# A half's second gather waits, in the GpSimd queue, for the half issued ahead of it to land

## The reference

```python
# each sample has 4096 past rows in 32 pages of a pool
phys = page_table[b4, start // PAGE_SIZE]
ks = jnp.where(is_past, pool_sk[phys[..., None], rows, g5], ...)
vs = jnp.where(is_past, pool_sv[phys[..., None], rows, g5], ...)
logits = einsum('btgrd,btgksd->btgrks', q, ks) * SM_SCALE + bias   # masked softmax
o_s    = einsum('btgrks,btgksd->btgrd', p, vs)
```

## Time and profile before

| | |
|---|---|
| median of 3 runs | 897.07 us (895.75 to 898.39) |
| profiled execution, its own time | 897.14 us |
| its span in the trace | 895.1 us |
| TensorE, VectorE, ScalarE, GpSimd busy | 96%, 69%, 42%, 14% |
| granted TensorE clock, mean | 0.994 of 2.4 GHz |
| DMA traffic | 118.31 MB, mean 132 GB/s |

### The profile page before, as it was taken

The page is one execution under the profiler, slowest core; times in us unless marked ns, Lnnn a source line. Parts: engine busy times, 40 slices in busy tenths (PEclk is TensorE's granted clock), DMA queues, the critical chain, the costliest instruction groups (busy, mean ns, idle before and its releaser), DMA issues.

```text
span 895.1 us, 15701 instructions
## 1 busy us (share of the span) xinstructions
PE 861.1 (96%) x6053; PEld 555.3 (62%) x6053; DVE 617.7 (69%) x1148; ACT 372.0 (42%) x885; POOL 121.7 (14%) x130
## 2 busy tenths in 40 slices
PE   9999999999999999999999998998889998999997
PEld 8656665666666666766775776766665766544442
DVE  5698789999988988999657557566766666222222
ACT  6111244211021211014877887776677666211111
POOL 1012110000001011110103131232244320000000
PEclk9999999999999999999999999999999999999999
DMA  9535551422144066630760020000019996521211
GB/s 327 188 118 169 188 206 55 61 50 76 43 135 182 27 208 227 212 126 40 250 227 25 11 86 2 1 1 2 1 53 378 415 416 267 178 84 65 83 70 36
DMA packets 32110, 118.31 MB, mean 132 GB/s; under 512 B 3434, under 2 KB 11772, under 8 KB 22972
## 3 DMA queue, kind: packets, MB, share of 16 engines
q0 software_dynamic: 9360, 68.16, 20.3%
q1 hardware_dynamic: 20316, 46.45, 15.1%
q10 hardware_dynamic: 2360, 2.71, 2.0%
HBM read 108.33 MB, written 13.29 MB: 136 GB/s over the span
## 4 chain that ended last, share of the span: by engine, by line
PE 89%; ACT 4%; DVE 3%; issue 2%; DVEq 1%; ACTq 0%; POOL 0%; POOLq 0%
PE PS L847 36%; PE PS L2210 12%; PE PS L1631 6%; PE PS L1641 6%; PE PS L1661 5%; PE PS L2029 3%; ACT main L1428 3%; PE PS L2090 2%; PE PS L2054 2%; PE PS L813 2%; PE PS L2067 2%; PE PS L829 1%; PE PS L1614 1%; DVE main L1474 1%; DVE main L1483 1%
## 5 line engine op out<-in xcount | busy, mean ns | idle before, releaser
L847 PE MATMUL PS<-main 128*128 128x352 f32 (+1 forms) x1056 | 327.9, 469 | 0.0
L847 PEld LDWEIGHTS PS<-main 128*128 128x128 f32 x1056 | 200.3, 191 | 119.5 <-issue 1.3
L1428 ACT ACTIVATE main<-PS,main 128x512 f32<-128x512 f32 (+3 forms) x192 | 103.8, 561 | 49.2 <-DVE main L1470 24.5
L2210 PE MATMUL PS<-main 128*128 128x512 f32 x256 | 111.6, 593 | 0.0
L434 ACT ACTIVATE main<-PS 128x384 f32<-128x384 f32 x24 | 11.7, 489 | 199.4 <-PE PS L847 195.5
L644 DVE SCALAR_TENSOR_TENSOR main<-main,par 128x1022 f32<-128x1022 f32 (+16 forms) x66 | 83.8, 1270 | 5.3 <-issue 0.4
L1641 PE MATMUL PS<-cst,main 128*128 128x128 f32 x528 | 73.2, 280 | 13.3 <-ACT main L1428 12.8
L2210 PEld LDWEIGHTS PS<-main 128*128 128x128 f32 x256 | 47.9, 190 | 58.1 <-issue 58.0
L603 DVE TENSOR_TENSOR main<-main 128x1024 f32<-128x1024 f32 x64 | 75.5, 1221 | 9.3 <-DMA main<-in_cmp_k_dram,row 6.5
L606 DVE TENSOR_TENSOR main<-main 128x1024 f32<-128x1024 f32 (+2 forms) x96 | 75.0, 781 | 7.2
L1641 PEld LDWEIGHTS PS<-cst,main 128*128 128x128 f32 x528 | 56.7, 140 | 29.7 <-ACT main L1428 23.6
(11 more groups left out here) (328 smaller groups left out, 1039.2 us busy)
## 6 DMA issues: line engine op xcount, KB each, us to landing
main<-in_w_tiles_dram SPq DMA_DIRECT2D x24, 512.0 KB, 3.6
out_dram<-main SPq DMA_DIRECT2D x18, 256.0 KB, 2.0
main<-in_x_prompt_dram SPq DMA_DIRECT2D x8, 512.0 KB, 8.6
main<-in_w_out_dram SPq DMA_DIRECT2D x4, 1024.0 KB, 7.8
main<-in_x_prompt_dram SPq DMA_DIRECT2D x16, 256.0 KB, 2.9
out_dram<-main SPq DMA_DIRECT2D x4, 512.0 KB
diag<-in_win_k_dram SPq DMA_DIRECT2D x8, 256.0 KB
diag<-in_win_v_dram SPq DMA_DIRECT2D x8, 256.0 KB, 7.8
```

The costliest lines, as they stand in the source:

```text
L847: last = pe.matmul(bank(3 * s + j)[:, 0:w], ring[:, s, k * P:(k + 1) * P], xT[:, k, t0:t0 + w], start=(k == 0), stop=(k == KD - 1))
L1428: last = act.activation(prob[:, k % 2, g, h * nk_ * P:(h + 1) * nk_ * P], score_set(k, g)[:, h * nk_ * P:(h + 1) * nk_ * P], ACT.Exp, scal ...
L2210: last = pe.matmul(out_bank(m, h), proj[:, MIX[k], n * P:(n + 1) * P], wo[:, k, h * 512:(h + 1) * 512], start=(x == 0), stop=(x == KD - 1))
```

## The change

From K11 on, every half's second gather (`b2 == 1`) waits until the half that stands ahead of it in the queue has landed, both of its gathers. The first gather of a half has no such wait. K00, K01, V00 and K10 stay as they were. The waits are on GpSimd's own queue, between a half's first and second gather.

```diff
-        def pool_keys(pool, pr, h):
+        def keys_landed(pr, h):
+            return kd_ld[h], 32 * pr + 32
+        def values_landed(p, h):
+            return (vd_ld[2], 32 * p + 32) if h else (vd_ld[p % 2], 32 * (p // 2) + 32)
+        def wait_gather(pool, ahead, b2):
+            if ahead is not None and b2 == 1:
+                pool.wait_ge(*ahead)
+        def pool_keys(pool, pr, h, ahead=None):
             for b2 in range(2):
+                wait_gather(pool, ahead, b2)
                 pool.indirect_dma_start(kd[:, b2, h * 2048:(h + 1) * 2048], None, half_rows("sel_k"),
...
-        def pool_values(pool, pr, h):
+        def pool_values(pool, pr, h, ahead=None):
             for b2 in range(2):
+                wait_gather(pool, ahead, b2)
...
         def pool_decode(pool):
-            def keys(pr, h):
+            def keys(pr, h, ahead):
                 keys_used(pool, pr - 1, 4 * h + 3)
-                pool_keys(pool, pr, h)
+                pool_keys(pool, pr, h, ahead)
...
-            keys(1, 1)
+            keys(1, 1, keys_landed(1, 0))
...
-            values(0, 1)
-            values(1, 0)
+            values(0, 1, keys_landed(1, 1))
+            values(1, 0, values_landed(0, 1))
             for pr in (2, 3):
-                keys(pr, 0)
-                values(pr, 0)
-                keys(pr, 1)
-                values(pr - 1, 1)
-            values(3, 1)
+                keys(pr, 0, values_landed(1, 0) if pr == 2 else values_landed(1, 1))
+                values(pr, 0, keys_landed(pr, 0))
+                keys(pr, 1, values_landed(pr, 0))
+                values(pr - 1, 1, keys_landed(pr, 1))
+            values(3, 1, values_landed(2, 1))
```

More of the change, by code:

```diff
@@ L1808, in pool_decode, with values @@
         def pool_decode(pool):
-            def keys(pr, h):
+            def keys(pr, h, ahead):
                 keys_used(pool, pr - 1, 4 * h + 3)
-                pool_keys(pool, pr, h)
-            def values(pr, h):
+                pool_keys(pool, pr, h, ahead)
+            def values(pr, h, ahead):
                 before = pr - 1 if h else pr - 2
@@ L1816, in values @@
                     values_used(pool, before, 4 * h + 3)
-                pool_values(pool, pr, h)
-            keys(1, 1)
+                pool_values(pool, pr, h, ahead)
+            keys(1, 1, keys_landed(1, 0))
             pool.wait_ge(SEM["oz"], NT)
```

## The result

The changed kernel takes 909.8 us (median of 4 runs, 904.6 to 910.9) against 896.8 us before. The ratio is 1.0138, 95% interval 1.012 to 1.0155: **slower by 1.4%**. The forecast was 897.2 us, in a range from 895.2 to 901.5; the time lies outside it. The profiled execution took 910.0 us, its span is 907.9 us, 12.8 us more than before.

A forecast was written before the change was run, and what follows sets the result against it. TensorE, busy 96% of the span, was taken to bound the kernel, with the DMA engines close to a bound in decode. 897.14 + 0.3 (K21) - 0.2 (unexplained pauses) = 897.2 us, range 895.2 to 901.5.

The forecast's parts named there:

- the pace above: Between the landings of K11 and K21 before the change: 2.86 us for a gather, 5.72 us for a half.
- the queue gets short but not empty, and the pace stays 5.72 us: Decode gathers: a new gather has data to move 1.6 us after the landing, within the 2.86 us of work ahead.
- first data after 1.3 us: From a gather's issue to its first data takes about 1.3 us, read at K10's first gather, issued at 669.20.
- The upper one, 6.2 us: Five halves to K21 at 5.9 + 0.3 us each: K21 lands at 716.2, cost 2.5 us.
- Rival 1: Decode: engines run dry between issues and K21 stalls TensorE; more than 2.7 us late above 6.24 us a half; chance 0.24.
- inside its slack: K31 another 1.6 us late at 6.8 us a half, less its slack of 3.3 us, so it costs nothing.
- priced at nothing: V21, like V11, K30, V30 and K31, costs nothing as long as K21 is at most 2 us late.
- its 902.6: Kernel time in us at 6.8 us a half: K21 lands at 719.2, 5.5 us late, and K31 adds nothing.
- The argument that the queue's depth covers it: The trace agrees with a fixed cost for each DMA, but had it covered by the queue's depth.
- The slack: Landing to TensorE's first use: K11 3.6 us, K20 1.8, K21 0.1, V11 3.2, K31 3.3.
- everything hung on K21: K21, with 0.1 us of slack, decides; all other halves have 1.8 us or more; K21 priced at +0.3 us.
- Rival 2: TensorE's five unnamed pauses, 7.0 us, are fetches queued behind gathers and shrink; to count, by half: 893.7 us; chance 0.11.

The follow-up runs named there:

- the repeat with the same ratio: The changed kernel, unchanged, on another chip, against the kernel before at 896.8 us there: 910.5 us, ratio 1.0137.
- the two variants for it: Against the kernel before, second gathers wait for the first gather of the half ahead: keys alone 896.6 us, ratio 1.0005; K11, V01, V10 alone 897.6 us, 1.0017.

## Why the prediction was wrong

**The step that failed** is this one: "When half N-1 has landed, N's first gather is on the engines, with 2.86 us of work at the pace above", and from it "the queue gets short but not empty, and the pace stays 5.72 us". The changed kernel's own windows around a landing refute it. K11 landed at about 690.1 and V01's second gather was issued at 690.34:

```profile
690.20:690.70 0.50, 0.50 (x17) 0.16 (x16) 0.41 (x1) 0.50 (x1) 0.36 (x1) 1.00 1.00 426
690.70:691.20 0.50, 0.50 (x16) 0.00 (x0) 0.50 (x1) 0.48 (x3) 0.50 (x1) 1.00 0.71 279
691.20:691.70 0.50, 0.50 (x44) 0.50 (x40) 0.40 (x2) 0.50 (x2) 0.20 (x2) 1.00 0.24 98
691.70:692.20 0.50, 0.50 (x45) 0.50 (x34) 0.49 (x1) 0.50 (x2) 0.50 (x1) 1.00 1.32 197
692.20:692.70 0.50, 0.50 (x18) 0.41 (x10) 0.39 (x4) 0.06 (x1) 0.32 (x1) 1.00 0.43 82
692.70:693.20 0.50, 0.50 (x6) 0.50 (x5) 0.50 (x1) 0.02 (x1) 0.00 (x0) 1.00 0.61 213
693.20:693.70 0.50, 0.50 (x7) 0.50 (x6) 0.11 (x2) 0.50 (x2) 0.00 (x0) 1.00 0.95 393
```

The rate begins to fall 0.4 us after the issue: V01's first gather was nearly through when K11's landing was told, not at its beginning with 2.86 us of work. And the new gather isn't at full rate when its first data moves, 1.4 us after the issue, but only near 693.2, 2.9 us after it. In between, 2.0 us run at a mean of (98 + 197 + 82 + 213) / 4 = 148 GB/s, not 415. That is 2.0 x (1 - 148 / 415) = 1.3 us of lost transfer at this landing, and the pace rose by 6.88 - 5.72 = 1.16 on the mean. The price of "first data after 1.3 us" was read right and used for the wrong thing.

The hole isn't the same behind every landing. Here are the stretches behind those of V01, V10, K20, V20 and K21:

```profile
697.50:699.50 2.00, 2.00 (x20) 2.00 (x20) 0.91 (x4) 1.45 (x3) 1.19 (x2) 1.00 0.74 197
704.00:705.00 1.00, 1.00 (x26) 0.22 (x24) 0.69 (x1) 1.00 (x3) 0.90 (x1) 1.00 0.70 172
711.00:714.00 3.00, 3.00 (x16) 2.85 (x15) 0.23 (x1) 1.79 (x3) 1.68 (x2) 0.50 0.63 162
717.00:719.00 2.00, 2.00 (x19) 2.00 (x20) 0.37 (x3) 1.44 (x3) 1.67 (x2) 1.00 0.97 387
724.50:727.50 3.00, 2.98 (x14) 2.98 (x15) 0.27 (x2) 1.32 (x3) 1.88 (x2) 0.50 0.47 107
```

There are three microseconds at 162 and 107 GB/s behind K20 and K21, and hardly a hole behind V20. Over all five halves, after and before, it comes out:

```profile
690.10:724.50 34.40, 27.62 (x592) 20.49 (x590) 19.75 (x52) 20.04 (x39) 9.40 (x10) 0.95 0.92 348
```

```profile
685.04:713.64 28.60, 27.11 (x600) 19.74 (x598) 18.42 (x46) 20.98 (x42) 9.05 (x10) 1.00 1.02 419
```

34.4 x (1 - 348 / 419) = 5.8 us, which is all of the 34.4 - 28.6 = 5.8 us that the five halves took longer. So the pace is lost transfer and nothing else.

**The bounds were too narrow.** The upper one, 6.2 us, took K11's 5.9 us for the most that a gather with one ahead takes. In the chain it is 5.7 for some and 7.7 for others, plus 0.26 for the release; K11's own second gather took 7.33. I guessed next that the 7.7 came of window loads on the same engines. Without the loads the mean stays at 6.7, so they may shift time between halves but aren't the cause of the pace. The rates tell a part of what sets 5.7 against 7.7: the stretches of K20 and K21 (7.9 us) ran at 385 and 406 GB/s, so the engines also moved what stood behind, and the deep holes are the ones that follow them. Why the landing comes late in these is open.

**Rival 1 was right in its mechanism and, for this trace, nearly in its size.** It put 6.8 us for a half (measured 6.9) and K21 5.5 us late; the waits for K20 and K21 were 3.5 + 2.65 = 6.1 us. It missed three terms. The clock after each pause, 3.4 us in all, was in no case's sum. K31 lost 0.7 where I had it inside its slack. V21, priced at nothing, lost 1.3: its second gather was issued at 751.5, not 731.4, and took 10.9 us to land beside the loads of the output weights. With these and the shorter pauses its 902.6 becomes 902.6 + 0.6 + 3.4 + 0.7 + 1.3 - 2.7 = 905.9; the profiled execution without the chance fall at the start would be 910.0 - 3.4 = 906.6. That the terms fit half by half is partly luck: in the repeat with the same ratio K21 cost 0.2 us and K31 7.6.

**The page of the Trainium skill** that spoke against the change, "DMA: Bandwidth & Descriptors", section "Anatomy of one DMA", gave, as an estimate, 6.8 us for a half when its fixed 2.0 us is exposed once. The trace has 6.9, but that it is so close is luck. The estimate is for a half that begins on an empty queue, with both gathers' bytes behind one fixed part. That is what the wait on the first gather made, and there a half took 9.8 us, 3.0 more than the estimate. In the changed kernel the next half's first gather had its start behind it, so its bytes weren't in the wait in full. What the page was right about is the direction: a fixed part came into the open. The argument that the queue's depth covers it was mine, and it holds from four gathers on, not for three.

**The slack was read rightly, but not everything hung on K21.** K21 had nothing to give, and with the waits only after K21 the loss was 0.2%, with those up to K21 0.5%. But TensorE's waits for gathers fell mostly on K20 and K21 in this trace, on K20 and K31 in the second, and on K21, K31 and V21 in a third. With a pace above TensorE's own 6.4 us for a half, K21 isn't the only half that can come late. Also right was where it would show: the DMA share below 0.95 (0.91 from 685 to 745; the sign of rival 1 was 0.9), K21 after 716, and gathers as what ended PE's idle time.

**Rival 2**, that the unnamed pauses shrink, came true in part: 7.0 to 4.3 us, where it asked for half. The shorter queue alone isn't the reason, for with four under way and no wait for gathers, on a chip of kind 1, they are 7.0 us again. On chips of kind 2 a shorter queue does go with less standing still: the long pause near 680 is gone where the burst is.

## What to carry to other kernels

A wait that throttles a queue of transfers costs nothing only while the work still to be moved when the landing is told lasts longer than the way from issue to full rate. That way was 2.8 to 2.9 us behind the landings of K11, K20 and K21, not the 1.3 us to the first data. Count the work from the landing, not from the plan: of the 1 MB gather behind the awaited one, little was left at these three landings. With 1 MB gathers and a need of 370 GB/s, three under way were too few here and four enough; and an engine whose stream is held up by a late transfer can pay a second time, with its clock.

## What the runs showed that I had not expected

- The clock can fall after short pauses: TensorE stood for 3.5 and 2.7 us and then had 1.2 GHz instead of 2.4 for over 3 us each time, which made the stalls of 6.1 us cost 9.5. It doesn't always: in the changed kernel's trace on a chip of kind 2 TensorE stood for 3.56 us up to 750.0, and the clock stayed at 2.4 GHz:

```profile
750.00:752.00 2.00, 1.98 (x18) 1.98 (x19) 0.00 (x0) 1.28 (x3) 0.94 (x1) 1.00 1.00 414
```

- The same kernel differs by 0.8% between chips (896 to 897 or 903 to 904 us), and the change's loss with it (1.4% or 0.6%). The changed kernel takes 909 to 911 us on all of them. The kernel before loses time on chips of kind 2, where ACT, DVE and PE stand still together for 4 to 5 us with no named cause, and the changed kernel has no such pause. So the ratio there is a loss and a gain in one. One comparison on one chip would have given half or twice the loss.
- Issuing fewer gathers at a time made a kernel faster on chips of kind 2: 0.4 to 0.6% with four under way. The traces tie the pause to the burst near 680. That the burst alone makes the gain wasn't tested there, as the two variants for it ran on a chip of kind 1.
